# Two transformer blocks on one core: other eviction counts, other places for hosted sums and latent pieces, and another form of the inverse roots

## The reference

```python
def rms_norm(x, g):
    return x * lax.rsqrt(jnp.mean(x * x, axis=-1, keepdims=True) + EPS) * g

for l in range(2):
    shift, scale, gate = jnp.split(silu(c) @ w_ada[l] + b_ada[l], 3, axis=-1)
    h = rms_norm(x, norm_g[l]) * (1.0 + scale) + shift            # the same for ctx
    q, k, v, g_gqa, cq, ckv, kr, g_mla = split(h @ w_in[l])
    q, k = rope(rms_norm(q)), rope(rms_norm(k))                   # GQA, 8 heads, 2 kv heads
    qm  = rms_norm(cq, cq_gain) @ w_uq                            # MLA, latent rank 512
    kvm = rms_norm(ckv, ckv_gain) @ w_ukv
    y = concat([attend(q, k, v) * silu(g_gqa), attend_mla(qm, kvm, kr) * silu(g_mla)])
    x = x + gate * (y @ w_out[l])                                 # ctx too in l0, not in l1
return rms_norm(x, final_g)
```

## Time and profile before

| | |
|---|---|
| median of 3 runs | 2957.47 us (2956.2 to 2958.33) |
| the profiled execution, its own time | 2954.25 us |
| its span | 2952.5 us |
| mean granted TensorE clock | 0.992 |
| PE busy | 2855.4 us, 97% of the span |
| DVE busy | 2050.1 us, 69% |
| ACT busy | 1247.2 us, 42% |
| POOL busy | 146.5 us, 5% |
| DMA | 589.44 MB, mean 200 GB/s |

### The profile page before, as it was taken

One profiled execution on the slowest core, in us unless ns is written; L12 is line 12 of the kernel. 1 busy time (PEld: TensorE's weight loads), 2 busy tenths in 40 slices (PEclk: granted clock), 3 DMA queues, 4 the chain that ended last, 5 costly groups with the idle time before them and its releaser, 6 DMA issues.

```text
span 2952.5 us, 38139 instructions
## 1 busy us (share of the span) xinstructions
PE 2855.4 (97%) x14299; PEld 2337.8 (79%) x14299; DVE 2050.1 (69%) x2936; ACT 1247.2 (42%) x2128; POOL 146.5 (5%) x229
## 2 busy tenths in 40 slices
PE   6999999998999999999999999999999999999998
PEld 2587678988778888887887889887888788888886
DVE  3368745837878889997895858873458677785466
ACT  3331435517454555454444332324444225445353
POOL 1100000001010000000000100000001001001000
PEclk9999999999999999999999999999999999999999
DMA  9877145841868778787886546772215565784333
GB/s 361 315 258 240 40 130 166 303 145 37 300 206 269 246 257 257 244 266 249 280 290 211 183 146 172 235 229 64 86 47 167 196 198 167 227 274 145 106 141 134
DMA packets 282822, 589.44 MB, mean 200 GB/s; under 512 B 31073, under 2 KB 64073, under 8 KB 278928
## 3 DMA queue, kind: packets, MB, share of 16 engines
q1 hardware_dynamic: 272240, 546.64, 56.4%
q0 software_dynamic: 10000, 39.72, 3.8%
q10 hardware_dynamic: 400, 0.66, 0.1%
HBM read 572.21 MB, written 14.72 MB: 199 GB/s over the span
## 4 chain that ended last, share of the span: by engine, by line
PE 77%; DVE 6%; ACT 3%; issue 2%; DMA 1%; POOL 0%; DVEq 0%; ACTq 0%; POOLq 0%
PE bank L3567 20%; PE bank L3569 20%; PE bank L3568 20%; PE bank L3577 2%; PE bank L3579 2%; PE bank L3578 2%; PE bank L1552 2%; DVE w_lo L3504 1%; PE bank L1543 1%; DVE acc L754 1%; ACT w_hi L3474 1%; PE bank L2602 1%; PE bank L1256 1%; DMA fin_g<-in_final_g 0%; DMA raw<-in_w_out 0%
## 5 line engine op out<-in xcount | busy, mean ns | idle before, releaser
L3504 DVE TENSOR_TENSOR w_lo<-raw,w_hi 128x1024 fp32r<-128x1024 f32 (+2 forms) x668 | 785.4, 1186 | 422.7 <-ACT w_hi L3474 406.2
L3474 ACT ACTIVATE w_hi<-raw 128x1024 fp32r<-128x1024 f32 (+2 forms) x668 | 680.6, 1031 | 927.2 <-PE bank L3569 650.1
L754 DVE SCALAR_TENSOR_TENSOR acc<-raw,sc_t,acc 128x1024 f32<-128x1024 f32 x480 | 601.2, 1279 | 34.4 <-DMA acc<-in_b_ada 28.4
L3567 PE MATMUL bank<-w_hi,l_hT_hi 128*128 128x512 f32 (+1 forms) x1056 | 389.6, 369 | 1.8 <-DVE l_hT_lo L1044 1.4
L3569 PE MATMUL bank<-w_hi,l_hT_lo 128*128 128x512 f32 (+1 forms) x1056 | 387.1, 367 | 0.0
L3568 PE MATMUL bank<-w_lo,l_hT_hi 128*128 128x512 f32 (+1 forms) x1056 | 386.9, 366 | 0.0
L3567 PE MATMUL bank<-w_hi,f_hT_hi 128*128 128x512 f32 x704 | 277.7, 394 | 1.4 <-DVE mod L802 1.1
L3569 PE MATMUL bank<-w_hi,f_hT_lo 128*128 128x512 f32 x704 | 274.6, 390 | 0.0
L3568 PE MATMUL bank<-w_lo,f_hT_hi 128*128 128x512 f32 x704 | 274.4, 390 | 0.0
L3567 PEld LDWEIGHTS bank<-w_hi,l_hT_hi 128*128 128x128 f32 x1056 | 198.3, 188 | 37.8 <-issue 6.3
L3569 PEld LDWEIGHTS bank<-w_hi,l_hT_lo 128*128 128x128 f32 x1056 | 198.2, 188 | 31.4
(11 more groups left out here) (495 smaller groups left out, 4609.5 us busy)
## 6 DMA issues: line engine op xcount, KB each, us to landing
raw<-in_w_in SPq DMA_DIRECT2D x240, 512.0 KB, 4.9
raw<-in_w_mod SPq DMA_DIRECT2D x192, 512.0 KB, 5.6
raw<-in_w_ada SPq DMA_DIRECT2D x192, 512.0 KB, 4.5
raw<-in_w_up SPq DMA_DIRECT2D x176, 512.0 KB, 4.8
raw<-in_w_out SPq DMA_DIRECT2D x96, 512.0 KB, 4.9
raw<-in_w_down SPq DMA_DIRECT2D x88, 512.0 KB, 5.6
raw<-in_w_in SPq DMA_DIRECT2D x32, 288.0 KB, 3.2
raw<-in_w_ukv SPq DMA_DIRECT2D x32, 256.0 KB, 3.5
```

The lines of the kernel that those rows point to most:

```text
L754: e.scalar_tensor_tensor(acc[a][:, :], raw[s % RAW_SLOTS][:, :], scalar, acc[a][:, :], ALU.mult, ALU.add).then_inc(fma_done, 1)
L3474: e.activation(slot(w_hi[u % SPLIT_SLOTS], g.width), slot(raw[s % RAW_SLOTS], g.width), ACT.Copy).then_inc(hi_ready, 1)
L3504: e.tensor_tensor(slot(w_lo[u % SPLIT_SLOTS], g.width), slot(raw[s % RAW_SLOTS], g.width), slot(w_hi[u % SPLIT_SLOTS], g.width).bitcast(F3 ...
L3567: e.matmul(o, xh[:, k, tok], hi[:, kk, :], start=first, stop=False)
```

## The change

1. `rsqrt`: the factor -0.5 goes into the seed, which takes two operations rather than three. For n > 2 each Newton step stays at three. For n <= 2 a step is two operations of one column each, `t = (y*y)*ms` with `y` as a scalar read from memory, and `y = (t+1.5)*y`; the columns are interleaved, and an operation waits only for its own column's predecessor.
2. The third and fourth sum hosted by l0's input projection start one unit earlier.
3. `FIRST` is 2 rather than 0 in l0: the nine latent pieces go with items 4 to 12 rather than 2 to 10.
4. The first sum hosted by l0's output projection has a span of 11 units rather than 12.
5. In the last output projection groups 0 and 1 get `leave_units = 3`, so that they are evicted one unit earlier; the final multiplication of both stands one unit later (units 15 and 23 rather than 14 and 22).

```diff
+        def rsqrt_seed(dve, ms, y, scale):
+            chain(dve, "dve", dve.tensor_scalar(ms, ms, -0.5 * scale, -0.5 * EPS, ALU.mult, ALU.add))
+            chain(dve, "dve", dve.tensor_scalar(y.bitcast(I32), ms.bitcast(I32), -0.5, float(0x5F3759DF - 2 ** 22 - 2 ** 30),
+                                                ALU.mult, ALU.add))
+
         def rsqrt_start(dve, ms, y, t, scale):
-            chain(dve, "dve", dve.tensor_scalar(ms, ms, scale, EPS, ALU.mult, ALU.add))
-            chain(dve, "dve", dve.tensor_scalar(y.bitcast(I32), ms.bitcast(I32), 1, None, ALU.logical_shift_right))
-            chain(dve, "dve", dve.tensor_scalar(y.bitcast(I32), y.bitcast(I32), -1.0, float(0x5F3759DF), ALU.mult, ALU.add))
+            rsqrt_seed(dve, ms, y, scale)
             rsqrt_steps(dve, ms, y, t, 1)
...
                 chain(dve, "dve", dve.tensor_tensor(t, y, y, ALU.mult))
-                chain(dve, "dve", dve.scalar_tensor_tensor(t, t, -0.5, ms, ALU.mult, ALU.mult))
+                chain(dve, "dve", dve.tensor_tensor(t, t, ms, ALU.mult))
                 chain(dve, "dve", dve.scalar_tensor_tensor(y, t, 1.5, y, ALU.add, ALU.mult))
 
         def rsqrt(dve, ms, y, t, scale):
-            rsqrt_start(dve, ms, y, t, scale)
-            rsqrt_steps(dve, ms, y, t, 2)
+            n = ms.shape[1]
+            if n > 2:
+                rsqrt_start(dve, ms, y, t, scale)
+                rsqrt_steps(dve, ms, y, t, 2)
+                return
+            rsqrt_seed(dve, ms, y, scale)
+            cols = [slice(i, i + 1) for i in range(n)]
+
+            def each(level, op):
+                for i, c in enumerate(cols):
+                    if level:
+                        dve.wait_ge(order["dve"], counts["dve"] - n + 1)
+                    counts["dve"] += 1
+                    op(c).then_inc(order["dve"], 1)
+
+            for step in range(3):
+                each(step, lambda c: dve.scalar_tensor_tensor(t[:, c], y[:, c], y[:, c], ms[:, c], ALU.mult, ALU.mult))
+                each(1, lambda c: dve.scalar_tensor_tensor(y[:, c], t[:, c], 1.5, y[:, c], ALU.add, ALU.mult))
+            dve.wait_ge(order["dve"], counts["dve"])
...
-                  hosts=None if last else [(5, 15), (24, 18), (47, 13), (63, 12)],
+                  hosts=None if last else [(5, 15), (24, 18), (46, 13), (62, 12)],
...
-            FIRST = 6 if last else 0
+            FIRST = 6 if last else 2
...
-                gemms(gs, sums_l1[1], hosts=[(2, 12), (18, 13)], hooks=join, ready=ready_cat)
+                gemms(gs, sums_l1[1], hosts=[(2, 11), (18, 13)], hooks=join, ready=ready_cat)
...
-                    hook(hooks, "dve", main_units(steps, 2, gs[i]), final(i))
+                    hook(hooks, "dve", main_units(steps, 2 if i == 2 else 4, gs[i]), final(i))
...
+            for g in gs[0:2]:
+                g.leave_units = 3
             gemms(gs, [], lead=6, hooks=fin_hooks, ready=ready_cat)
```

## The result

The changed kernel took 2962.58 us (median of 15 runs, 2959.48 to 2967.3), the kernel before beside it 2956.41 (15 runs, 2950.21 to 2958.33). The ratio is 1.0027, 95% interval 1.002 to 1.0034: about 8 us slower where 5 us less were forecast (the two medians alone stand 6.2 apart). The profiled execution has a span of 2965.5 us (before 2952.5) at a granted clock of 0.991; at 2967.3 us it is the slowest of the fifteen, so the two spans must not be subtracted.

A forecast was written before the change was run, and what follows sets the result against it. PE, busy 97% of the span, was taken to bound the kernel. Roots -2.6, handover -0.2, pieces -0.2, l0's output projection -4.0, last projection +1.9 gave -5.1: 2952.4 us against the median, 8 in 10 between 2948.8 and 2956.8.

The forecast's parts named there:

- DVE's splits run well ahead of PE: 0: l0's input projection: moving the third sum's multiply-adds one unit earlier costs nothing, as DVE's splits are ahead; 0 us.
- Last projection, +1.9: Last output projection: earlier eviction waits for `fin_g`, so unit 11's `w_lo` is 3.9 late; +1.9 us, bounds +0.9 and +2.9.
- Latent pieces, -0.2: l0's attention: the 1.80 wait goes, -1.9, and two pieces cost 1.7 at items 11 and 12; net -0.2, range -1.5 to +1.
- the same two pieces then cost 2 x 0.86: l0's attention: the two pieces removed in front cost 0.86 us each, 1.7 together, at items 11 and 12.
- l0's output projection, -4.0: The late `w_lo` stall goes whole: 2.02 delay, 1.7 slow clock, 0.3 at the turn; -4.0 us.
- The wait of 1.06 for `raw` should be absorbed: Start of l0's output projection: this DVE wait vanishes, so `w_lo` is there at 2312.05, 0.65 us before PE wants it.
- the rival I gave 0.12: l0's output projection: two more pairs and a late `raw` make unit 11's `w_lo` late; -4.7 to +0.6 us; chance 0.12.
- Roots, -2.6: Shorter inverse roots on PE's path: pre1 -1.1, pre2 -0.7, last eviction -0.6, n = 16 one -0.2; sum -2.6 us.
- the second rival: Roots: the two columns' operations don't overlap, so the whole change gives -1.4 us, 2956.1; chance 0.13.
- Handover, -0.2: Input projection to attention: the fourth sum's earlier turn takes copies from the first item's front; at most -0.2 us of 1.62.
- the first rival: Last projection costs nothing or pieces come free at items 11 and 12: -6.4 to -7.0 us, 2950.5 to 2951.1; chance 0.25.
- the upper bound of the last projection: Last output projection: `fin_g` lands no sooner and the slow clock lasts longer; +2.9 us.

## Why the prediction was wrong

The forecast was -5.1 us, the measurement about +8 (ratio 1.002 to 1.0034, 5.9 to 10 us). Undoing one part at a time gives, in ratio: part 5 0.0014, part 2 0.0013, part 3 0.0002, part 4 -0.0003; the roots alone give -0.0002. The sum is 0.0024, within the interval of the whole, but each term is uncertain by about 0.001. By stages, as an estimate from the table and the experiments: roots -1.1, input projection +2.9 to +4.7 and -0.2 at the handover, pieces +1.9, output projection -0.8, last projection +3.2, together +6 to +8. The forecast was off by 3 to 5 us in the third sum, 1.6 to 3.2 in l0's output projection, 2.1 in the pieces, 1.5 in the roots and 1.3 in the last projection.

- **Third sum, "DVE's splits run well ahead of PE: 0".** This step failed. I looked at PE's waits before (none) and not at what stood between the sum's first multiply-add and the split: DVE already waited 1.82 for the bias, behind the split of unit 47. The move puts that wait and 5 us of multiply-adds ahead of the split. Instead of 0 it measured +2.9, and +4.7 where the slow clock followed (+3.8 by time). I had given it no range at all.
- **Last projection, +1.9.** The mechanism was right and the size was off: a delay of 4.5 to 5.2 at unit 11 (forecast 3.9) and about 2.4 of slow clock in unit 11 against 1.7 in unit 12. `fin_g` landed no sooner, where I had given it 0.7 to 0.9. The stage went up 3.2 to 3.7, beyond the upper bound of 2.9.
- **Latent pieces, -0.2.** That "the same two pieces then cost 2 x 0.86" failed. The removed wait (1.80) left room for two others (0.6 more for `l_gq_lo`, 0.4 for `l_gP`), so the front won 1.0 and not 1.9; the ninth piece met the key transposes, and the stretch behind took 2.9 more and not 1.7, 1.4 of it a wait that no row before showed. +1.9 in the stage, beyond the upper bound of 1.
- **l0's output projection, -4.0.** The late stall went as forecast (-2.1). The slow clock behind it, which I counted in full (1.7), is there in two of seven profiles. "The wait of 1.06 for `raw` should be absorbed" failed: with the DMA full the wait stayed (1.12) and another of 1.12 came up in front of it, and unit 11 was 1.2 to 2 late. This is the rival I gave 0.12, in a milder size. Net -0.8 by stage with the clock up on both sides, -2.4 against the profile of before; the -0.9 by time is within its noise.
- **Roots, -2.6.** The durations were right within 0.07. The last eviction won its 0.58 in full, the n = 16 one about 0.15. In pre1 0.95 was won from the wait and 0.85 lost behind it, and in pre2 0.67 and about 0.4. That makes -1.1: the step that failed is that a wait cut short is won in full. By time -0.6, with an interval of 2.6 either way. The rule of the Trainium skill, "VectorE: DVE Perf Modes", The DRAIN you can't avoid, that the next operation doesn't start until the pipe is empty, would make fourteen operations longer than twelve. The same section says that a next operation that is not held starts earlier, and the pairs agree with that: 0.35 for two of 0.21. So the second rival took the section's rule without its exception.
- **Handover, -0.2.** 3.33 to 3.12 from matmul 9525 to 9533: right.
- **The range.** Its ends don't follow from the terms named beside them: both gains of the first rival make -8.3, that is 2949.2 and not 2948.8, and the second rival with the upper bound of the last projection -0.4, 2957.1 and not 2956.8. That changes nothing: 2962.58 lies outside either.

## What to carry to other kernels

Before moving work earlier in an engine's queue, find the last operand that it waits for and ask whether that can come earlier as well; if it can't, everything behind it is moved later. A wait of an engine that no other engine is seen to wait for (DVE's 1.82 for the bias) is a reserve only while it stands behind what others need. An eviction that waits on one count for two loads should wait only for what it reads: by stage the kernels with a semaphore of its own for `fin_g` win 3.8 of their 6 us in the last projection, 1.7 of that by the clock, more than any reordering brought. No run has this semaphore alone on the kernel before.

## What the runs showed of the hardware

Of a wait of PE that is shortened without falling away, little may be left. In pre1 0.95 less waiting was followed by 0.85 more in the matmuls behind, 0.8 of it lost at the granted clock of 0.50, as means of nine profiles against five that overlap in part. Also, behind a wait of 1.90 in the input projection the clock fell to 0.50 in two profiles and stayed at 1.00 in a third, and behind 1.61 to 1.86 in l0's output projection (span 12) it fell in two of seven (5.48 us for 17 matmuls against 3.88). So such a loss is to be counted as a chance, not in full. What of the activity before decides it stays open.

Tiny DVE operations that wait only for the one before the last overlap: with a scalar read from memory the two columns' operations take 0.27 together (842.87 to 843.14), hardly more than the 0.25 of one.
